# Sample rows of a MoE block spread over 128 partitions and gathered by two row halves of TensorE

## The chip, the cores and the metric

The kernel runs on one core of a Trainium2 chip. The metric is the device time of one execution in microseconds. The kernel before took 584.08, 584.25 and 587.18 us in three timed runs, median 584.25.

## The reference

One inference step of a two-layer decoder trunk on 256 prompt tokens and 64 sample tokens (8 sequences of 8), model width 1024, everything float32. Layer 0 mixes by sliding-window attention and a diagonal state space model, layer 1 by a gated recurrence and dilated attention. Each layer ends in the same block, a hierarchical mixture of experts over the 320 token rows:

```python
def hier_moe(x, p):                       # x: normed rows, 320 x 1024
    g_idx = argmax(x @ router_g + b_g)    # one of 4 groups
    e_in  = logits of the 4 experts of that group
    top_v, top_i = top_k(e_in, 2)         # 2 of 16 experts for each row
    hid = silu(x @ w_gate[e]) * (x @ w_up[e])     # 1024 -> 256
    y   = sum over the two experts of gate * (hid @ w_down[e])   # 256 -> 1024
```

The change lies in this block alone, and the block runs once in each layer.

## The kernel before

The token rows lie in three tiles: t = 0 and 1 are the prompt's (128 rows each), t = 2 the samples' (64 rows, `ROWS[2]`). `moe_block` has one program for each engine, written out by hand; semaphores alone order them.

- **Norm and store (ScalarE, L1743 to L1752).** For each tile ScalarE squares the residual rows with a sum (L1745), takes the root (L1748), waits for VectorE's reciprocal (L1829), scales the rows into `xn` (L1750) and stores them in DRAM as `x_rows` by one DMA of its own queue (L1752): 128 rows of 4 KB for t = 0 and 1, 64 rows of 4 KB for t = 2. Landings are counted by `first_out` (t = 0 and 1) and `rows_out` (t = 2).
- **Routing (VectorE, TensorE).** Logits, choice of two experts, place of each row in its expert's list of 64 (`CAP`). `place(0, 2)` and `place(2, 3)` (L1911, L1914) write the one-hot matrix `Sf` for the first two experts.
- **First pair of experts.** The 16 experts are worked in 8 pairs j = 0 to 7, 64 rows for each expert of a pair. The rows of pair 0 don't come from DRAM: `gather_first` (L1489) multiplies `xn` by `Sf`, eight products for each tile, all three tiles summed in banks 2 and 3 of PSUM. VectorE moves each bank out with the norm's gain (`first_turned`, L1849) to `xgT`.
- **up, turn_hidden, down.** `up(j)` (L1518) multiplies `xgT` by gate and up weights, two experts side by side on column halves of TensorE, into bank 2 + j % 2. `down(j)` (L1549) writes banks 4 and 5.
- **List of the other pairs.** After `up(0, 0, 2)` TensorE makes the row lists of all pairs (L1618) from `L` (VectorE, L1939) and `H` (GpSimd, L1415). VectorE writes them out as `idx` (L1949). GpSimd then fetches the rows of pair 1 from `x_rows` (`gather(1)`, L1400), which `turn(1)` (L1500) transposes. Before it GpSimd waits for `first_out`, `rows_out`, `idx_ok` and `first_pe`. In layer 0 `turn(1)` comes right after `up(0)`, in layer 1 after `down(0)` (`TURN_LATE`).
- **Weights.** SyncE loads pieces of 1 MB (L1273) as places come free. In the first pair it also waits for `gather_steps`, which GpSimd raises right behind `gather(1)`.

TensorE's queue is in order, so a wait in it holds all that follows:

```python
gather_first(2)
up(0, 0, 2)
pe.wait_ge(H_ok, 1)
pe.wait_ge(S_ok, 1)
...                      # the lists, L1618
up(0, 2, KC)
```

Of the kernel before, what the change touches and what calls it, by code (L numbers as in the profile page):

```python
# [16 lines left out]
P = 128  # L17
# [1169 lines left out]
def moe_block(c, x, layer, parts, items, zeroed, xnT, copies, n_copies):  # L1187
# [52 lines left out]
    def gathered_rows(j):  # L1240

        return m["xg"][(j - 1) % XG]

    def yo_of(j):

        return yo[j // LAST]
# [58 lines left out]
    with nc.Block(no_gpsimd_drain=True) as block:  # L1305
# [88 lines left out]
        @block.gpsimd  # L1394
        def _(pool):
            nc.gpsimd.memset(xn[64:P, 2], 0.0).then_inc(gather_steps, 1)

            def gather(j):

                pool.indirect_dma_start(out=gathered_rows(j), out_offset=None, in_=x["x_rows"],  # L1400
                                        in_offset=bass.IndirectOffsetOnAxis(ap=gather_idx[:, j:j + 1], axis=0),
                                        bounds_check=TOK - 1, oob_is_err=False).then_inc(c.xg_in[(j - 1) % XG], 16)

            def scatter(j):

# [12 lines left out]
            pool.wait_ge(first_out, 32)  # L1418
            pool.wait_ge(rows_out, 16)
            pool.wait_ge(idx_ok, 1)  # L1420
            pool.wait_ge(first_pe, 3)
            gather(1)
            nc.gpsimd.memset(m["zero"][:, 1:2], 0.0).then_inc(gather_steps, 1)
            for j in range(2, 1 + XG):
                gather(j)
            pool.wait_ge(zeroed, 16)
            for j in range(LAST):
                if 1 + XG + j < PAIR_N:
                    pool.wait_ge(xt_pe, j + 1)
                    gather(1 + XG + j)  # L1430
                if j < LAST - 1:
                    scatter(j)

        @block.tensor
        def _(pe):
# [50 lines left out]
            def gather_first(t, first=0, end=KC):  # L1486

                for q in range(first, end):
                    last = nc.tensor.matmul(c.bank[2 + q // 4][:, (q % 4) * P:(q % 4 + 1) * P], xn[0:ROWS[t], t, q * P:(q + 1) * P],  # L1489
                                            m["Sf"][0:ROWS[t], t].rearrange("p e s -> p (e s)"),  # L1490
                                            start=(t == 0 and q % 4 == 0), stop=(t == 2 and q % 4 == 3))
                    if t == 2 and q % 4 == 3 or t == 0 and q == KC - 1:
                        last.then_inc(first_pe, 1)

            def turn(j):

                gathered(pe, j)
                pe.wait_ge(xt_ok, 2 * j)
                for q in range(KC):
# [4 lines left out]
            def up(j, first, end):  # L1504

                w = [[piece(6 * j + 2 * part + i).rearrange("p (k n) -> p k n", n=2 * FF) for part in range(2)] for i in range(2)]
                if first == 0:
                    piece_arrived(pe, 6 * j)
                    piece_arrived(pe, 6 * j + 1)
                    pe.wait_ge(xt_ok, 2 * j + 1)  # L1510
                for q in range(first, end):
                    if q == KC // 2:
                        pe.wait_ge(xt_ok, 2 * j + 2)
                        piece_arrived(pe, 6 * j + 2)
                        piece_arrived(pe, 6 * j + 3)
                    for i in range(2):
                        half = slice(64 * i, 64 * i + 64)
                        last = nc.tensor.matmul(c.bank[2 + j % 2][half, :], xgT[:, j % 2, q, half], w[i][q // 4][:, q % 4, :],  # L1518
                                                start=(q == 0), stop=(q == KC - 1))
# [221 lines left out]
        def _(act):  # L1741
            act.dma_start(m["route_in"], x["route_in"][layer]).then_inc(ld, 16)
            for t, rows in enumerate(ROWS):  # L1743
                act.wait_ge(added, 2 * t + 2)
                nc.scalar.activation(xn[0:rows, t], c.resid[0:rows, t], ACT.Square,  # L1745
                                     accum_out=c.stat[0:rows, t:t + 1]).then_inc(sq_ok, 1)
# [3 lines left out]
                nc.scalar.activation(xn[0:rows, t], c.resid[0:rows, t], ACT.Copy, scale=c.stat[0:rows, 6 + t:7 + t]).then_inc(xn_ok, 1)  # L1750
                act.wait_ge(xn_ok, t + 1)
                act.dma_start(x["x_rows"][t * P:t * P + rows, :], xn[0:rows, t]).then_inc(rows_out if t == 2 else first_out, 16)  # L1752
            act.wait_ge(earg, 1)
# [3 lines left out]
            for j in range(PAIR_N):  # L1757
                act.wait_ge(up_pe, j + 1)
                if j >= 2:
                    act.wait_ge(hid_ok, j - 1)  # L1760
                nc.scalar.activation(sg[:, j % 2], c.bank[2 + j % 2][:, 0:FF], ACT.Silu).then_inc(sg_ok, 1)  # L1761
                act.wait_ge(ht_pe, j + 1)
# [52 lines left out]
        def _(dve):  # L1815
# [29 lines left out]

            def first_turned(h):

                dve.wait_ge(first_pe, h + 2)
                v.tensor_tensor(xgT[:, 0, 4 * h:4 * h + 4, :], c.bank[2 + h][:, :].rearrange("p (k r) -> p k r", k=4),  # L1849
                                c.gains[:, gain, 4 * h:4 * h + 4].unsqueeze(2).broadcast_to([P, 4, P]), ALU.mult).then_inc(xt_ok, 1)  # L1850

# [56 lines left out]
            def place(a, b):  # L1908

                dve.wait_ge(pos_pe, 1 + a // 2)  # L1910
                v.scalar_tensor_tensor(m["tmp"][:, a:b], c.bank[7][:, 16 * a:16 * b].rearrange("p (t e) -> p t e", e=E_N), 1.0,  # L1911
                                       m["sum"][:, a:b], ALU.add, ALU.mult).then_inc(tmp_ok, 1)
                dve.wait_ge(tmp_ok, 1 + a // 2)
# [49 lines left out]
            def hidden(j):  # L1963

                dve.wait_ge(sg_ok, j + 1)
                if j >= 2:
                    dve.wait_ge(ht_pe, j - 1)
                v.tensor_tensor(hid[:, j % 2], sg[:, j % 2], c.bank[2 + j % 2][:, FF:2 * FF], ALU.mult).then_inc(hid_ok, 1)  # L1968

# [972 lines left out]
```

## Time and profile before

| | before |
|---|---|
| median of three timed runs | 584.25 us (584.08, 584.25, 587.18) |
| profiled execution, its own time | 586.33 us |
| its span | 584.1 us |
| TensorE busy | 558.7 us, 96% |
| VectorE, ScalarE, GpSimd busy | 247.0, 155.9, 89.0 us |
| moved by DMA | 208.94 MB, mean 358 GB/s |

The profile is of one execution, whose own time is 2.2 us longer than the span of its instructions. "Busy" is time in which an engine works. A released wait is shown in brackets behind the instruction that it held: the idle time, and who ended it. Line numbers are those of the kernel before.

### The profile page before, as it was taken

The page shows a single profiled execution, that of the slowest core. Times are in us where ns is not written, and L with a number is a line of the kernel's source. Part 1 is how long each engine was busy: PE and PEld are TensorE (multiplying, and loading weights), DVE is VectorE, ACT ScalarE, POOL GpSimd, SP SyncE. Part 2 cuts the span into 40 slices and gives each one's busy share as a digit, 9 for nine tenths or more (in the row PEclk, how much of TensorE's full clock was granted, in tenths as well). Part 3 has the DMA queues.
Part 4 walks back from the last instruction along what each step waited for, and adds up shares of the span by engine and source line. Part 5 has one row for each costly group of instructions (what it writes and reads, how often), then busy time and mean ns, then how long its engine had stood idle before and what let it go on. Part 6 is the DMA issues. An engine that isn't in the chain of part 4 may idle for free. (4 is left out here: it accounts for less than half of the span.)

```text
span 584.1 us, 8477 instructions
## 1 busy us (share of the span) xinstructions
PE 558.7 (96%) x3422; PEld 307.2 (53%) x3422; DVE 247.0 (42%) x558; ACT 155.9 (27%) x328; POOL 89.0 (15%) x116
## 2 busy tenths in 40 slices
PE   5999999999999999998999999999999889999993
PEld 4777876544533333337876556567644533333331
DVE  6999882224651112145633415250113732221146
ACT  7132295121301101134235105163013210101123
POOL 5993800000121110000100001000000012120000
PEclk9999999999899999999999999999999999999997
DMA  8995999996999999999999998999699999999872
GB/s 328 418 358 78 239 390 382 383 417 272 378 388 421 420 421 418 397 295 376 380 416 328 412 397 297 313 354 422 257 421 420 381 364 415 420 420 422 363 235 91
DMA packets 40073, 208.94 MB, mean 358 GB/s; under 512 B 12835, under 2 KB 14563, under 8 KB 24192
## 3 DMA queue, kind: packets, MB, share of 16 engines
q1 hardware_dynamic: 30560, 169.93, 74.5%
q0 software_dynamic: 7872, 34.53, 16.5%
q10 hardware_dynamic: 1600, 3.90, 1.7%
q8 instruction: 29, 0.48, 0.3%
q14 instruction: 12, 0.10, 0.0%
HBM read 198.77 MB, written 43.74 MB: 415 GB/s over the span
## 5 line engine op out<-in xcount | busy, mean ns | idle before, releaser
L1518 PE MATMUL bank<-arena 128*64 128x512 f32 x264 | 87.1, 610 | 0.5 <-DVE arena L1858 0.5
L1518 PE MATMUL bank<-ring,arena 128*64 128x512 f32 x232 | 76.3, 613 | 0.1
L2315 PE MATMUL bank<-arena,ring 128*128 128x320 f32 x256 | 71.6, 434 | 0.0
L2315 PEld LDWEIGHTS bank<-arena,ring 128*128 128x128 f32 x256 | 48.0, 190 | 21.4 <-issue 1.6
L1439 PE MATMUL bank<-ring,arena 128*128 128x512 f32 x92 | 40.3, 594 | 1.0 <-PEq L455 0.6
L1518 PEld LDWEIGHTS bank<-arena 128*64 128x64 f32 x264 | 24.2, 138 | 31.9 <-issue 31.8
L1549 PE MATMUL bank<-arena 128*64 128x512 f32 x136 | 39.8, 594 | 0.7 <-ACT arena L1763 0.7
L577 PE MATMUL bank<-xnT,ring 128*128 128x320 f32 x144 | 39.5, 434 | 0.6 <-DVE xnT L897 0.6
L1974 DVE COPY arena<-bank 128x512 f32<-128x512 f32 x14 | 9.7, 692 | 68.3 <-PE bank L1549 68.3
L1549 PE MATMUL bank<-ring,arena 128*64 128x512 f32 x120 | 36.1, 593 | 0.7 <-ACT arena L1763 0.7
L1518 PEld LDWEIGHTS bank<-ring,arena 128*64 128x64 f32 x232 | 21.1, 139 | 25.2 <-issue 25.0
L577 PEld LDWEIGHTS bank<-xnT,ring 128*128 128x128 f32 x144 | 27.1, 190 | 11.7 <-DVE xnT L897 0.7
L1439 PEld LDWEIGHTS bank<-ring,arena 128*128 128x128 f32 x92 | 17.2, 190 | 22.7 <-issue 22.7
L1761 ACT ACTIVATE arena<-bank 128x256 f32<-128x256 f32 x16 | 6.1, 384 | 84.6 <-PE bank L1518 84.6
L1408 POOL DMA_INDIRECT y_rows<-arena x12 | 12.1, 1007 | 107.2 <-DVE arena L1974 107.2
L1968 DVE TENSOR_TENSOR arena<-arena,bank 128x256 f32<-128x256 f32 x16 | 6.7, 422 | 49.0 <-ACT arena L1761 49.0
L1858 DVE TENSOR_TENSOR arena<-bank,small 128x512 f32<-128x512 f32 x28 | 18.0, 686 | 22.1 <-PE bank L1500 19.6
L1766 ACT COPY arena<-bank 128x512 f32<-128x512 f32 x16 | 9.4, 586 | 65.0 <-PE bank L1549 65.0
L1549 PEld LDWEIGHTS bank<-arena 128*64 128x64 f32 x136 | 12.4, 136 | 20.7 <-issue 20.1
L2371 PE MATMUL bank<-ring,arena 128*128 128x512 f32 (+1 forms) x64 | 21.2, 489 | 0.0
L1745 ACT ACTIVATE arena<-resid 128x1024 f32<-128x1024 f32 (+1 forms) x6 | 6.3, 1058 | 54.0 <-DVE resid L1824 54.0
L1549 PEld LDWEIGHTS bank<-ring,arena 128*64 128x64 f32 x120 | 11.4, 136 | 16.1 <-issue 15.7
(450 smaller groups left out, 851.7 us busy)
## 6 DMA issues: line engine op xcount, KB each, us to landing
arena<-in_w_moe SPq DMA_DIRECT2D x50, 1024.0 KB, 16.4
ring<-in_w_moe SPq DMA_DIRECT2D x44, 1024.0 KB, 15.0
arena<-in_stream_b SPq DMA_DIRECT2D x4, 2560.0 KB, 15.0
out_o_d_old<-in_cache_d_g POOLq DMA_DIRECT2D x1, 8448.0 KB, 29.8
arena<-in_stream_a SPq DMA_DIRECT2D x4, 2048.0 KB, 10.4
out_o_d_old<-in_cache_d_g POOLq DMA_DIRECT2D x1, 7680.0 KB, 40.7
out_o_d_old<-in_cache_d_g SPq DMA_DIRECT2D x1, 4608.0 KB, 38.2
ring<-in_w_out_even SPq DMA_DIRECT2D x2, 2048.0 KB, 11.2
```

What stands on the lines that cost most here:

```text
L577: last = nc.tensor.matmul(bank(name)[:, 0:TOK], lhs(k), c.xnT[:, k, :], start=(k == 0), stop=(k == KC - 1))
L1408: pool.indirect_dma_start(out=x["y_rows"], out_offset=bass.IndirectOffsetOnAxis(ap=scatter_idx[:, j:j + 1], axis=0), in_=yo_of(j), in_offs ...
L1439: last = nc.tensor.matmul(c.bank[2 * t + h][:, :], parts[q][:, t * P:(t + 1) * P], where[q][:, h * 512:(h + 1) * 512], start=(q == 0), sto ...
L1518: last = nc.tensor.matmul(c.bank[2 + j % 2][half, :], xgT[:, j % 2, q, half], w[i][q // 4][:, q % 4, :], start=(q == 0), stop=(q == KC - 1))
L1549: last = nc.tensor.matmul(c.bank[4 + h][half, :], hidT[:, j % 2, f, half], w[i][:, f, h * 512:(h + 1) * 512], start=(f == 0), stop=(f == 1))
L1745: nc.scalar.activation(xn[0:rows, t], c.resid[0:rows, t], ACT.Square, accum_out=c.stat[0:rows, t:t + 1]).then_inc(sq_ok, 1)
L1766: nc.scalar.copy(yo_of(j)[:, 0:512], c.bank[4][:, :]).then_inc(yo_a, 1)
L1858: v.tensor_tensor(xgT[:, j % 2, 4 * h:4 * h + 4, :], c.bank[h][:, :].rearrange("p (k r) -> p k r", k=4), c.gains[:, gain, 4 * h:4 * h + 4] ...
L1968: v.tensor_tensor(hid[:, j % 2], sg[:, j % 2], c.bank[2 + j % 2][:, FF:2 * FF], ALU.mult).then_inc(hid_ok, 1)
L1974: v.tensor_copy(yo_of(j)[:, 512:D], c.bank[5][:, :]).then_inc(yo_b, 1)
L2315: last = nc.tensor.matmul(bank(name)[:, 0:TOK], w[:, k, i * P:(i + 1) * P], xnT[:, k, :], start=(k == 0), stop=(k == KC - 1))
L2371: last = nc.tensor.matmul(bank(f"v{2 * t + n}")[:, 0:m], xnT[:, k, t * P:(t + 1) * P], wv[:, k, c0:c0 + m], start=(k == 0), stop=(k == KC ...
```

## The change

The samples' 64 normed rows are no longer 64 partitions of 1024 columns: the first 512 columns stand on partitions 0 to 63 and the last 512 on partitions 64 to 127, both in columns 0 to 511 of `xn[:, 2]`. `tmp` and with it `Sf[:, 2]` get a copy on partitions 64 to 127. `gather_samples` takes the place of `gather_first(2)`: the same eight products, but in pairs, one on the upper and one on the lower 64 rows of TensorE, for bank 2 and bank 3. The square goes to `xgT`, the scaling is two instructions of 64 x 512, and the store is two DMAs of 64 rows of 2 KB. `first_turned` is in three parts (columns 0 to 1, 2 to 3, 4 to 7 of eight), and the first of them releases `up(0, 0, 2)`, which now writes bank 4.

```diff
-            nc.gpsimd.memset(xn[64:P, 2], 0.0).then_inc(gather_steps, 1)
+            nc.gpsimd.memset(xn[:, 2], 0.0).then_inc(gather_steps, 1)
...
-            pool.wait_ge(rows_out, 16)
+            pool.wait_ge(rows_out, 32)
...
+    def up_bank(j):
+        return 2 + j % 2 if j else 4
...
+            def gather_samples():
+                for q in range(4):
+                    for h in range(2):
+                        half = slice(64 * h, 64 * h + 64)
+                        last = nc.tensor.matmul(c.bank[2 + h][:, q * P:(q + 1) * P], xn[half, 2, q * P:(q + 1) * P],
+                                                m["Sf"][half, 2].rearrange("p e s -> p (e s)"), start=False, stop=(q == 3))
+                        if q == 3:
+                            last.then_inc(first_pe, 1)
...
                 if first == 0:
-                    pe.wait_ge(xt_ok, 2 * j + 1)
+                    pe.wait_ge(xt_ok, 2 * j + 2 if j else 1)
                 for q in range(first, end):
+                    if j == 0 and q == 2:
+                        pe.wait_ge(xt_ok, 2)
...
-            pe.wait_ge(xn_ok, 3)
-            gather_first(2)
+            pe.wait_ge(xn_ok, 4)
+            gather_samples()
...
+                else:
+                    act.wait_ge(gather_steps, 1)
+                    for h in range(2):
+                        nc.scalar.activation(xn[64 * h:64 * h + 64, 2, 0:512], c.resid[0:64, 2, h * 512:(h + 1) * 512], ACT.Copy,
+                                             scale=c.stat[0:64, 8:9]).then_inc(xn_ok, 1)
+                    act.wait_ge(xn_ok, 4)
+                    for h in range(2):
+                        act.dma_start(x["x_rows"][SEQ:TOK, h * 512:(h + 1) * 512], xn[64 * h:64 * h + 64, 2, 0:512]).then_inc(rows_out, 16)
...
+            v.memset(m["tmp"][64:P, 2], 0.0)
...
+                if a == 2:
+                    v.scalar_tensor_tensor(m["tmp"][64:P, 2, 0:2], c.bank[7][0:64, 32:34], 1.0, m["sum"][0:64, 2, 0:2], ALU.add, ALU.mult)
...
-            first_turned(0)
-            first_turned(1)
+            first_turned(0, 2)
+            first_turned(2, 4)
+            first_turned(4, KC)
```

## Rows read from the trace of the kernel before

**Rows 1.** The page: the span, and busy time of each engine.
```profile
span 584.1 us, 8477 instructions
PE 558.7 (96%) x3422; PEld 307.2 (53%) x3422; DVE 247.0 (42%) x558; ACT 155.9 (27%) x328; POOL 89.0 (15%) x116
```

**Rows 2.** Timeline, layer 0: start us, length us, engine, line; idle time before it.
```profile
152.04 2.05 PE L1489 MATMUL bank<-arena 64*128 64x128 f32 x16 [0.68 <-DVE arena L1914]
153.30 1.51 DVE L1849 TENSOR_TENSOR arena<-bank,small 128x512 f32<-128x512 f32 x2 [0.39 <-PE bank L1489]
154.73 0.95 DVE L1939 TENSOR_TENSOR arena<-arena 128x768 bf16<-128x768 f32 x1
...
157.96 0.17 DVE L1949 TENSOR_SCALAR arena<-bank 128x16 uint32<-128x16 f32 x1 [1.32 <-PE bank L1618]
159.16 1.12 POOL L1400 DMA_INDIRECT arena<-x_rows,arena  x1 [6.83 <-issue]
163.16 0.86 PEld L1500 LDWEIGHTS bank<-ident,arena 128*128 128x128 f32 x8 [0.81 <-DMA arena<-x_rows,arena]
```

**Rows 3.** Timeline of PE alone, 153 to 164 us.
```profile
154.14 3.36 PE L1518 MATMUL bank<-arena 128*64 128x512 f32 x8
157.43 0.49 PE L1618 MATMUL bank<-arena 128*128 128x16 bf16 x12
157.85 5.38 PE L1518 MATMUL bank<-arena 128*64 128x512 f32 x24
```

**Rows 4.** PE in stretches: busy us, count, granted clock, DMA share, GB/s.
```profile
154.50:157.90 3.40, 3.40 (x22) 0.50 1.02 427
465.20:468.60 3.40, 3.35 (x9) 0.51 1.03 431
473.50:476.60 3.10, 1.44 (x8) 1.00 1.01 418
```

**Rows 5.** Chain that ended last, layer 1: start us, length us, what.
```profile
463.18 2.05 PE bank L1489 x16
465.28 3.53 PE bank L1518 x8
468.81 0.39 PE bank L1618 x12
```

**Rows 6.** Timeline, layer 1.
```profile
465.87 0.95 DVE L1939 TENSOR_TENSOR arena<-arena 128x768 bf16<-128x768 f32 x1
480.19 1.09 PE L1500 MATMUL bank<-ident,arena 128*128 128x128 f32 x8
```

**Rows 7.** Timeline: 64-row products in two row halves, and small operations.
```profile
67.80 1.16 PE L647 MATMUL bank<-arena 64*128 64x128 f32 x16
147.15 0.76 DVE L1836 TENSOR_TENSOR xnT<-bank,small 128x256 f32<-128x256 f32 x2 [0.55 <-PE bank L1458]
141.99 0.26 DVE L1894 SCALAR_TENSOR_TENSOR arena<-arena 128x16 f32<-128x16 f32 x2
148.34 1.15 ACT L1750 ACTIVATE arena<-resid,stat 64x1024 f32<-64x1024 f32 x1 [0.23 <-DVE stat L1829]
149.52 0.51 ACTq L1752 DMA_DIRECT2D x_rows<-arena  x1
169.04 0.59 ACT L1766 COPY arena<-bank 128x512 f32<-128x512 f32 x1 [3.95 <-PE bank L1549]
```

**Rows 8.** DMA issues at 125, 149.5 and 159 us: KB, us to landing.
```profile
x_rows<-arena ACTq DMA_DIRECT2D x1, 512.0 KB, 8.6
...
x_rows<-arena ACTq DMA_DIRECT2D x1, 256.0 KB, 7.3
...
arena<-x_rows,arena POOLq DMA_INDIRECT x1, 3.9
```

**Rows 9.** DMA queues, 153.4 to 156.9 us: packets, MB, share of 16 engines.
```profile
q1 hardware_dynamic: 164, 1.21, 82.2%
q10 hardware_dynamic: 80, 0.26, 18.5%
```

More of the change, by code:

```diff
@@ L1488, in gather_first @@
                 for q in range(first, end):
[L1489 to L1492, printed above, removed]
+                    last = nc.tensor.matmul(c.bank[2 + q // 4][:, (q % 4) * P:(q % 4 + 1) * P], xn[:, t, q * P:(q + 1) * P],
+                                            m["Sf"][:, t].rearrange("p e s -> p (e s)"), start=(t == 0 and q % 4 == 0), stop=False)
+                    if t == 0 and q == KC - 1:
                         last.then_inc(first_pe, 1)
+            def gather_samples():
[6 more added lines that the diff above has]
+                            last.then_inc(first_pe, 1)
             def turn(j):
                 gathered(pe, j)
-                pe.wait_ge(xt_ok, 2 * j)
+                pe.wait_ge(xt_ok, 2 * j + 1)
                 for q in range(KC):
@@ L1509, in up @@
                     piece_arrived(pe, 6 * j + 1)
-                    pe.wait_ge(xt_ok, 2 * j + 1)
+                    pe.wait_ge(xt_ok, 2 * j + 2 if j else 1)
                 for q in range(first, end):
+                    if j == 0 and q == 2:
+                        pe.wait_ge(xt_ok, 2)
                     if q == KC // 2:
-                        pe.wait_ge(xt_ok, 2 * j + 2)
+                        pe.wait_ge(xt_ok, 2 * j + 3)
                         piece_arrived(pe, 6 * j + 2)
@@ L1517, in up @@
                         half = slice(64 * i, 64 * i + 64)
-                        last = nc.tensor.matmul(c.bank[2 + j % 2][half, :], xgT[:, j % 2, q, half], w[i][q // 4][:, q % 4, :],
+                        last = nc.tensor.matmul(c.bank[up_bank(j)][half, :], xgT[:, j % 2, q, half], w[i][q // 4][:, q % 4, :],
                                                 start=(q == 0), stop=(q == KC - 1))
@@ L1744, in _ @@
                 act.wait_ge(added, 2 * t + 2)
-                nc.scalar.activation(xn[0:rows, t], c.resid[0:rows, t], ACT.Square,
+                nc.scalar.activation(xn[:, t] if t < 2 else xgT[0:64, 0].rearrange("p k m -> p (k m)"), c.resid[0:rows, t], ACT.Square,
                                      accum_out=c.stat[0:rows, t:t + 1]).then_inc(sq_ok, 1)
@@ L1749, in _ @@
                 act.wait_ge(rstd_ok, t + 1)
-                nc.scalar.activation(xn[0:rows, t], c.resid[0:rows, t], ACT.Copy, scale=c.stat[0:rows, 6 + t:7 + t]).then_inc(xn_ok, 1)
-                act.wait_ge(xn_ok, t + 1)
-                act.dma_start(x["x_rows"][t * P:t * P + rows, :], xn[0:rows, t]).then_inc(rows_out if t == 2 else first_out, 16)
+                if t < 2:
+                    nc.scalar.activation(xn[:, t], c.resid[:, t], ACT.Copy, scale=c.stat[:, 6 + t:7 + t]).then_inc(xn_ok, 1)
+                    act.wait_ge(xn_ok, t + 1)
+                    act.dma_start(x["x_rows"][t * P:(t + 1) * P, :], xn[:, t]).then_inc(first_out, 16)
+                else:
[6 more added lines that the diff above has]
+                        act.dma_start(x["x_rows"][SEQ:TOK, h * 512:(h + 1) * 512], xn[64 * h:64 * h + 64, 2, 0:512]).then_inc(rows_out, 16)
             act.wait_ge(earg, 1)
@@ L1760, in _ @@
                     act.wait_ge(hid_ok, j - 1)
-                nc.scalar.activation(sg[:, j % 2], c.bank[2 + j % 2][:, 0:FF], ACT.Silu).then_inc(sg_ok, 1)
+                nc.scalar.activation(sg[:, j % 2], c.bank[up_bank(j)][:, 0:FF], ACT.Silu).then_inc(sg_ok, 1)
                 act.wait_ge(ht_pe, j + 1)
@@ L1844, in logits_out, with first_turned @@
                 v.tensor_copy(m["lgT"][:, t * P:t * P + ROWS[t]], c.bank[5][:, t * P:t * P + ROWS[t]]).then_inc(lt_ok, 1)
[L1846 to L1850, printed above, removed]
+            def first_turned(k0, k1):
+                dve.wait_ge(first_pe, 2 + k0 // 4)
+                v.tensor_tensor(xgT[:, 0, k0:k1, :], c.bank[2 + k0 // 4][:, k0 % 4 * P:(k0 % 4 + k1 - k0) * P].rearrange("p (k r) -> p k r", r=P),
+                                c.gains[:, gain, k0:k1].unsqueeze(2).broadcast_to([P, k1 - k0, P]), ALU.mult).then_inc(xt_ok, 1)
             def xg_turned(j):
@@ L1910, in place @@
                 dve.wait_ge(pos_pe, 1 + a // 2)
-                v.scalar_tensor_tensor(m["tmp"][:, a:b], c.bank[7][:, 16 * a:16 * b].rearrange("p (t e) -> p t e", e=E_N), 1.0,
-                                       m["sum"][:, a:b], ALU.add, ALU.mult).then_inc(tmp_ok, 1)
+                if a == 2:
+                    v.scalar_tensor_tensor(m["tmp"][64:P, 2, 0:2], c.bank[7][0:64, 32:34], 1.0, m["sum"][0:64, 2, 0:2], ALU.add, ALU.mult)
+                rows = P if a == 0 else 64
+                v.scalar_tensor_tensor(m["tmp"][0:rows, a:b], c.bank[7][0:rows, 16 * a:16 * b].rearrange("p (t e) -> p t e", e=E_N), 1.0,
+                                       m["sum"][0:rows, a:b], ALU.add, ALU.mult).then_inc(tmp_ok, 1)
                 dve.wait_ge(tmp_ok, 1 + a // 2)
@@ L1967, in hidden @@
                     dve.wait_ge(ht_pe, j - 1)
-                v.tensor_tensor(hid[:, j % 2], sg[:, j % 2], c.bank[2 + j % 2][:, FF:2 * FF], ALU.mult).then_inc(hid_ok, 1)
+                v.tensor_tensor(hid[:, j % 2], sg[:, j % 2], c.bank[up_bank(j)][:, FF:2 * FF], ALU.mult).then_inc(hid_ok, 1)
             def pair_end(j):
```

## The prediction

> **What bounds the kernel now.** I read the page's busy times first: TensorE works 558.7 of 584.1 us [rows 1], and it is one queue in order, so what moves a waiting point of it moves the end. The chain that ended last, in order of time, confirms it for layer 1: samples' gather, `up(0, 0, 2)`, the lists, the rest of `up(0)`, one behind the other [rows 5]. Then I read the timeline of the same stretch in layer 0 [rows 2, 3], the stretches with their granted clock [rows 4], and last the DMA issues [rows 8, 9].
>
> Three things are to be seen there.
> - The samples' gather is 16 matmul records in 2.05 us, started by `Sf` (L1914). VectorE begins on bank 2 at 153.30, when half of them are done, and `up(0)` starts at 154.14 [rows 2, 3].
> - The first 8 records of `up(0)` take 3.36 us in layer 0 and 3.53 us in layer 1 [rows 3, 5]. Twenty-four take 5.38, that is 0.435 us for each of 12 pairs once the last record's 0.59 is off. Eight should take 4 x 0.435 + 0.15 = 1.9. The granted clock was 0.50 there, the lower of the two levels (1.2 against 2.4 GHz), right behind the 64-row gather [rows 4]. The gather itself had no break. In another stretch, 473.50 to 476.60, it was busy only 1.44 of 3.10 us and kept 1.00 [rows 4].
> - In layer 0 `turn(1)` is released by the landing of `gather(1)`: issued 159.16, 3.9 us to landing, 163.1, and TensorE's first weight load of it is at 163.16 [rows 2, 8]. TensorE itself was ready at the same moment (the last of 12 pairs starts at 157.85 + 11 x 0.435 = 162.6, and 0.55 later is 163.2). So there are two chains with no slack between them. In layer 1 `turn(1)` is at 480.19 [rows 6]; the rows are there by 468.8 + 5.7 = 474.5, with 5.7 the distance from lists to landing in layer 0.
>
> **The state of the timed runs.** The profiled execution took 586.33, 2.1 above the median, and the three runs are two near 584.2 and one 587.18. The half clock costs 1.46 us in layer 0 (4 x 0.435 after 154.14 less one pair, 155.44, plus 0.53 to the lists gives 155.97, against 157.43) and 1.65 in layer 1 (465.28 and the same 1.83 give 467.11; the chain has the lists from 468.81, shown some 0.05 late) [rows 3, 5]. Together 3.1 us, and 587.18 less 584.17 is 3.0. I take it that two of the three runs had full clock there and one had not. That is inference: no row shows an unprofiled run's clock. The sum is made for both.
>
> **The change part by part.**
>
> *Gather in halves.* The row for it is L647: 16 records of the same form, 64 rows by 128 columns, on two row halves and two banks, in 1.16 us [rows 7]. So 2.05 becomes 1.16, that is 0.89 less. If halves did not overlap it would stay 2.05, and both banks would end late (rival 4). But `up(0)` doesn't wait for the end of the gather, only for bank 2 and its evacuation: bank 2 is now whole some 1.1 us after the start instead of 1.2. So about 0 is gained here by itself; what goes is TensorE's own end at 154.09, which would have held any earlier `up`.
>
> *Evacuation in three.* The first part is 128 x 256 instead of 128 x 512. Two of 128 x 256 take 0.76, so 0.38 to 0.42 each, against 1.51/2 = 0.755 [rows 2, 7]: `up(0)` is released 0.35 earlier. The three together take 0.4 + 0.4 + 0.75 = 1.55 against 1.51, so VectorE goes on to `L` 0.04 later. The second part is there 0.4 behind the first; `up(0, 0, 2)` needs 1.9, so it hides it. The bank change (4 for 2) only lets this overlap be; bank 4 is read out long before.
>
> *The copy of `tmp`.* One more small operation ahead of L1911: two such take 0.26 where a small one by itself takes 0.17 (L1949) [rows 2, 7], so 0.09 on the path to `Sf`. It delays gather, evacuation and `L`. The memset of `tmp` is smaller still and stands far ahead, where VectorE waits for logits; with no such cover it would be 0.1 more.
>
> *ScalarE.* One scaling of 1.15 becomes two of 64 x 512; the nearest row is 0.59 for 128 x 512 [rows 7]. So 1.18, and `xn` is ready at 149.6, 2.4 us before TensorE asks for it. The square in `xgT` costs nothing, nor does the wait for a memset that is first in GpSimd's program. The second store's issue is at most 0.5 more of ScalarE's queue [rows 7], and the next there, an Exp, waits for VectorE's work behind `L`.
>
> Sum to the lists: `up(0)` starts 0.35 - 0.09 = 0.26 to 0.28 earlier with the bank's small gain. At half clock the lists follow `up`, so 0.28 a layer. At full clock they would follow `L` instead: before, `up` lets them start at 155.97 while `L` ends at 154.73 + 0.95 = 155.68; after, `up` gives 155.69 and `L`, 0.13 later, 155.81 and a release of 0.05. The gain is then only 0.12 a layer. In layer 1 the numbers are 467.11 against 466.95 [rows 6], so again about 0.12 to 0.15.
>
> *The store in two.* The 64 rows are now 128 pieces of 2 KB in place of 64 of 4 KB, on the same queue. Bytes are equal, so the lower bound is 0. For the upper: in 153.4 to 156.9 the store's queue (q10) held 18.5% of 16 engines for 80 packets, 64 of them of 4 KB, which makes 0.16 us each; q1 with 82.2% for 164, some 16 of them tiny, 0.31 each [rows 9]. If an engine takes the two queues in turn, each of the store's pieces costs 0.16 + 0.31 = 0.47, four for each engine now. Four more turns at that are 1.9. At 2 KB (0.08 + 0.31) eight turns are 3.1 against 1.9, and one more completion write, 0.3: 1.5. The nearest rows are the landings under load: 128 rows of 4 KB took 8.6, 64 rows 7.3 [rows 8], 1.3 for four more turns. I take 1.3.
>
> What it is worth: before, `rows_out` was whole at 149.52 + 7.3 = 156.8, and `idx` was written at 157.96 + 0.17 = 158.13; GpSimd's fetch started 1.03 later. So it was hidden by 1.3 us. After, it lands at 158.1 to 158.2 in both states.
> - Half clock: `idx` at 157.85, fetch at 158.13 + 1.03 = 159.16, as before. Layer 0 gains nothing: the 0.28 of `up` turns into a wait of `turn(1)`. Layer 1 keeps its 0.28. Sum 586.33 - 0.28 = 586.05.
> - Full clock: before, `idx` at 156.67 and rows at 156.8, fetch 157.8, landed 161.75, TensorE ready at 161.70: a tie. After, landed 163.1, TensorE ready at 161.6 and idle 1.5 us. Layer 0 loses 1.35. Layer 1 gains 0.12 (its `turn(1)` has 5 us of room, and the late landing costs nothing). Sum +1.2: 584.25 + 1.2 = 585.45.
>
> The wait added (`rows_out` 32 for 16) stands in GpSimd's queue ahead of `gather(1)`, of `gather_steps`, for which SyncE's weight loads of the first pair wait, and of `gather(2)`. These slide by 1.3 too at full clock; `turn(2)` slides with them, and the weights so loaded are pieces 19 and on, for pair 3 and later.
>
> The Trainium skill ("DMA: Bandwidth & Descriptors", Queues, rings and completion order) says that a DMA engine drains a whole packet of some 9 to 17 descriptors from one ring before it turns to the next. By that the store's smaller pieces would go out together and little would be added; the measured landings above, 1.3 later for four more pieces an engine, stand between this and strict turns. It is weighed as rival 1.
>
> **The rivals.**
> 1. *The store lands no later* (under 0.3). For: same bytes, and the second issue, 0.5 at most, may be hidden in the 7.3 to landing. Against: the 1.3 between 128 and 64 rows. Then full clock gives 0.12 + 0.12: 584.0; half clock 586.33 - 0.56. Chance 0.23.
> 2. *The clock stays up where it fell.* The fall came right behind 2.05 us of matmuls on half of the rows; now both halves work together, and `up` starts sooner. If the median run had the fall in it after all (the profile has), layer 1 keeps 1.63 and 0.12 in place of 0.28; layer 0 is bound by the store and gains nothing. Sum 584.25 - 1.75 = 582.5; with rival 1 too, -3.3 = 580.9. For: both falls stand behind that gather and none behind longer idle time. Against: the spread of the three runs. Chance 0.15.
> 3. *The clock falls in more runs* (the slower side). TensorE now idles: 0.9 less work in the gather, and at full clock 1.5 us before `turn(1)`, followed by a stretch of transposes and waits up to `down(0)`. If the clock falls in the median run where it did not, at two places, it is 1.2 + 3.1 = 4.3, 588.5; at one, 1.2 + 1.6, 587.05. [...] Against: one stretch with less than half busy kept 1.00 [rows 4]. The Trainium skill ("TensorE: Matmul & The Clock Gate", Part 1) ties the clock to how busy the engine was, and names idle stretches alone as the danger; by that the shorter gather would speak for this rival, but here the fall came behind a stretch busy throughout. Chance 0.12.
> 4. *The halves don't overlap.* Bank 2 whole at 154.2, `up` at 154.7: 0.55 later in each layer. With the store: 584.25 + 1.35 + 0.55 = 586.1. Against: L647. Chance 0.04.
>
> The forecast, the store's landing taking the place of the lists in layer 0, has the remaining 0.46.
>
> **How the numbers follow.** Likeliest 585.4, its own range 584.6 (store 0.5 later) to 586.2 (store 1.9 later, at full clock). The whole range 582.4 to 587.0 leaves out the far part of rivals 2 and 3. A change below 0.5%, 2.9 us, is about what a measurement of this kernel can't tell from none, so the bounds are 581.3 and 587.2. Faster needs rivals 2 and 1 together, or both falls gone: 0.06. Slower needs rival 3 at two places or beside another mishap: 0.09. The rest, 0.85, is no change that can be told.
>
> **What would show it.** The gather 16 records in 1.2 us, and L1849 in three instructions with the first near 0.4. `up(0)` about 0.28 us nearer to the row of L1911 than before. Landings of the two stores near 8 to 9 us after issue, `gather(1)` 1 us behind the later one and not behind `idx`, and in layer 0 `turn(1)` released by its DMA with a gap of over 1 us on TensorE if the clock is 1.00 before it. I am wrong if the stores land within 7.5 us, or if the stretch behind the gather is at 1.00 in the profile and the span has dropped by over 2 us.

## The result, and the profile after

| | before | after |
|---|---|---|
| median | 583.74 us (581.97 to 587.18, 10 runs) | 588.38 us (585.42 to 590.76, 10 runs) |
| profiled execution, its own time | 586.33 us | 588.18 us |
| its span | 584.1 us | 586.2 us |

The ratio is 1.0068 [1.005, 1.0086]: slower by 0.7%, and the median lies above the forecast range, which ended at 587.0. (In brackets behind a ratio stands its 95% interval.) Two more series of the changed kernel gave 1.0080 [1.0052, 1.0109] and 1.0045 [1.0022, 1.0069]. The mean of its 28 runs in all three series is 587.75 us, that of the 111 runs of the kernel before that were taken beside the experiments is 584.41, so the change costs 3.3 us where 1.2 was forecast. The mean granted clock of these runs is 0.9935 before and 0.9909 after. One run of one version below (after_4k_delay_both, 594.64 us) was in a slower state and is left out of its ratio and its clock.

The page after, against [rows 1]: TensorE has 2.7 us less work, and the span is 2.1 us longer.

```profile
span 586.2 us, 8489 instructions
PE 556.0 (95%) x3422; PEld 306.4 (52%) x3422; DVE 247.8 (42%) x564; ACT 156.4 (27%) x330; POOL 86.8 (15%) x116
```

The timeline of the changed kernel in layer 0, against [rows 2, 3, 7] (start us, length us, engine, line; in brackets the idle time before it and who ended it):

```profile
148.90 1.47 ACT L1772 ACTIVATE arena<-resid,stat 64x512 f32<-64x512 f32 x2 [0.23 <-DVE stat L1853]
150.40 1.15 ACTq L1776 DMA_DIRECT2D x_rows<-arena  x2
152.39 0.38 DVE L1942 TENSOR_TENSOR arena<-arena 128x128 f32<-128x128 f32 x1
152.83 1.16 PE L1503 MATMUL bank<-arena 64*128 64x128 f32 x16 [0.91 <-DVE arena L1942]
154.09 1.35 DVE L1873 TENSOR_TENSOR arena<-bank,small 128x256 f32<-128x256 f32 x3 [0.40 <-PE bank L1503]
154.66 1.94 PE L1533 MATMUL bank<-arena 128*64 128x512 f32 x8 [0.67 <-DVE arena L1873]
...
157.17 0.16 DVE L1978 TENSOR_SCALAR arena<-bank 128x16 uint32<-128x16 f32 x1
159.71 1.12 POOL L1404 DMA_INDIRECT arena<-x_rows,arena  x1 [6.81 <-DMA x_rows<-arena]
```

The gather takes 1.16 us, the first products of `up(0)` 1.94 at full clock, and `idx` is written at 157.33. `gather(1)` starts 2.4 us later, at 159.71, and what ended its idle time is the store. The later of the two stores landed at 158.79; in the kernel before, all rows were there at 156.78.

Layer 1 has the same wait, and the transposes of `turn(1)` (L1513) come long behind it, with TensorE busy ahead of them:

```profile
471.93 1.10 POOL L1404 DMA_INDIRECT arena<-x_rows,arena  x1 [6.13 <-DMA x_rows<-arena]
...
480.66 1.09 PE L1513 MATMUL bank<-ident,arena 128*128 128x128 f32 x8
```

The same line in the kernel before, released by `idx`:

```profile
470.39 1.10 POOL L1400 DMA_INDIRECT arena<-x_rows,arena  x1 [6.69 <-DVE arena L1949]
```

PE in stretches, changed kernel, against [rows 4] (stretch, its length, PE busy, granted clock, DMA share, GB/s):

```profile
154.50:157.90 3.40, 3.24 (x26) 1.00 1.02 421
263.30:265.20 1.90, 0.47 (x4) 1.00 1.05 448
265.30:268.60 3.30, 3.30 (x12) 0.50 0.78 335
467.20:469.20 2.00, 1.87 (x8) 1.00 1.01 410
```

Both falls behind the gather are gone (154.5 and 467.2 at 1.00), and there is a new one at 265.3. That is the start of the next norm, where TensorE had waited for ScalarE: 0.47 us of work in the 1.9 us ahead of it. Beside such stretches every execution has half clock in its last 4 to 10 us; that tail is not counted as a fall below.

**The measure that made the rest readable.** Span against span says little here, since a fall of the clock moves it as much as the change does. I cut each profiled execution at five events instead: r, the first product of the out projection, in layer 0 and 1 (L1439 before, L1443 after); g, the start of `gather(1)`; s, the first transposes of the next norm (L1680, L1695); and the end. All in us:

| | r to g, layer 0 | g to s | s to r | r to g, layer 1 | g to end |
|---|---|---|---|---|---|
| before | 46.14 (half clock) | 105.42 | 162.31 | 43.50 (half clock) | 113.76 |
| after | 46.13 | 105.58 | 163.75 (half clock) | 42.88 | 114.32 |
| before_three_parts | 44.97 | 105.47 | 162.78 | 41.93 | 113.91 |
| after_4k_store | 44.78 | 105.34 | 162.17 | 41.92 | 113.69 |
| before_delay_l1 | 44.86 | 105.21 | 162.54 | 44.61 (half clock) | 114.41 |
| before_delay_both | 45.73 | 105.25 | 163.27 | 42.93 | 114.65 |
| after_four_stores | 48.89 | 107.00 (half clock) | 162.16 | 45.70 | 116.98 |

"Half clock" marks a piece with a stretch of it in that execution. What is to be seen: from `gather(1)` to the end of the layer is nearly fixed, 105.2 to 105.6 and 113.7 to 114.7 (105.05 to 106.1 and 113.67 to 114.65 over all executions but those of experiments 3, 4 and 7), whatever the clock did before it, save where the gather is very late. So the end of each layer follows the start of `gather(1)`; experiments 7 and 8 test whether it is the cause. The profiled execution of the kernel before has its gather as late as the changed kernel in layer 0 (46.14), since `up(0)` ran at half clock there.

### The profile page after: what moved, and what is told of

The parts are those of the page before. It is cut to its first block and busy times, and to the rows that moved or that the text cites. A ratio compares the mean times of both kernels' runs of the same rounds, so it can differ in the third digit from the quotient of the medians.

```text
span 586.2 us, 8489 instructions
## 1 busy us (share of the span) xinstructions
PE 556.0 (95%) x3422; PEld 306.4 (52%) x3422; DVE 247.8 (42%) x564; ACT 156.4 (27%) x330; POOL 86.8 (15%) x116
## 5 line engine op out<-in xcount | busy, mean ns | idle before, releaser
L1533 PE MATMUL bank<-arena 128*64 128x512 f32 x264 | 85.6, 598 | 1.1 <-DVE arena L1873 0.7
L1533 PE MATMUL bank<-ring,arena 128*64 128x512 f32 x232 | 74.7, 598 | 0.7 <-DVE arena L1873 0.7
L1443 PE MATMUL bank<-ring,arena 128*128 128x512 f32 x92 | 40.3, 594 | 1.0 <-PEq L455 0.6
L1564 PE MATMUL bank<-arena 128*64 128x512 f32 x136 | 39.8, 594 | 0.7 <-ACT arena L1787 0.7
L1564 PE MATMUL bank<-ring,arena 128*64 128x512 f32 x120 | 36.1, 593 | 0.7 <-ACT arena L1787 0.7
L1443 PEld LDWEIGHTS bank<-ring,arena 128*128 128x128 f32 x92 | 17.2, 190 | 22.7 <-issue 22.7
```

Source lines behind the costliest of these rows:

```text
L1443: last = nc.tensor.matmul(c.bank[2 * t + h][:, :], parts[q][:, t * P:(t + 1) * P], where[q][:, h * 512:(h + 1) * 512], start=(q == 0), sto ...
L1533: last = nc.tensor.matmul(c.bank[up_bank(j)][half, :], xgT[:, j % 2, q, half], w[i][q // 4][:, q % 4, :], start=(q == 0), stop=(q == KC - 1))
L1564: last = nc.tensor.matmul(c.bank[4 + h][half, :], hidT[:, j % 2, f, half], w[i][:, f, h * 512:(h + 1) * 512], start=(f == 0), stop=(f == 1))
```

## Experiments

**1. The store by itself.** Kernel before, with only the samples' store in two:

```diff
-            pool.wait_ge(rows_out, 16)
+            pool.wait_ge(rows_out, 32)
...
+                    for h in range(2):
+                        act.dma_start(x["x_rows"][SEQ:TOK, h * 512:(h + 1) * 512], xn[0:64, 2, h * 512:(h + 1) * 512]).then_inc(rows_out, 16)
```

> The kernel before with one edit: the samples' 64 normed rows are stored by two DMAs of 64 rows of 2 KB instead of one of 64 rows of 4 KB. Store theory (the later landing holds gather(1): in layer 0 it holds TensorE at turn(1), in layer 1 it holds the weight loads behind gather(1), whose stream ends last): later store lands 1.3 to 1.6 us later than in the kernel before, gather(1) some 1.3 us later in layer 0 and 0.9 in layer 1 where the clock is 1.00, time +1.5 to +2.5 us. Clock theory (what costs is the half clock that falls in other places since the gather is shorter): the gather is as before, so no change, within 0.7 us. VectorE theory (the copy of tmp and three parts): no change.

586.87 us, ratio 1.0036 [1.0013, 1.0059], mean clock 0.9912. That is 2.1 us above the kernel before by the ratio and 2.6 by the medians, for the store alone. The rows are there at 158.20 in place of 156.78. Its `gather(1)` in layer 0 has the same releaser as after:

```profile
159.12 1.12 POOL L1400 DMA_INDIRECT arena<-x_rows,arena  x1 [6.81 <-DMA x_rows<-arena]
```

**2. Everything but the split store.** The changed kernel, with the samples' rows scaled whole on 64 partitions, stored by one DMA of 4 KB rows, and the second half scaled once more onto partitions 64 to 127:

```diff
-                    act.wait_ge(xn_ok, 4)
-                    for h in range(2):
-                        act.dma_start(x["x_rows"][SEQ:TOK, h * 512:(h + 1) * 512], xn[64 * h:64 * h + 64, 2, 0:512]).then_inc(rows_out, 16)
+                    nc.scalar.activation(xn[0:64, 2], c.resid[0:64, 2], ACT.Copy, scale=c.stat[0:64, 8:9]).then_inc(xn_ok, 1)
+                    act.wait_ge(xn_ok, 3)
+                    act.dma_start(x["x_rows"][SEQ:TOK, :], xn[0:64, 2]).then_inc(rows_out, 16)
+                    nc.scalar.activation(xn[64:P, 2, 0:512], c.resid[0:64, 2, 512:D], ACT.Copy, scale=c.stat[0:64, 8:9]).then_inc(xn_ok, 1)
```

> The changed kernel with the store of before: ScalarE scales the 64 rows at full width onto partitions 0 to 63, stores them by one DMA of 64 rows of 4 KB, and then scales columns 512 to 1023 once more onto partitions 64 to 127 for the lower row half. Gather in halves, evacuation in three and the copy of tmp stay. Store theory: gather(1) goes back behind idx, time within 0.7 us of the kernel before (583.2 to 584.4), perhaps 0.3 below. Clock theory: stays near 588.4, since the gather is still 1.16 us. VectorE theory: stays near 588.4.

584.94 us, 1.0013 [0.9997, 1.0029], clock 0.9932. The row halves, the copy of `tmp` and the three parts cost nothing that can be told, and bring nothing either. `gather(1)` starts 2.1 us earlier than after, still released by the rows, which here landed at 156.71; the next norm has 0.79 us of idle time ahead where the changed kernel has 1.52, and the clock did not fall in this execution before its tail.

```profile
157.62 1.12 POOL L1404 DMA_INDIRECT arena<-x_rows,arena  x1 [5.47 <-DMA x_rows<-arena]
262.96 1.09 PE L1695 MATMUL bank<-ident,arena 128*128 128x128 f32 x8 [0.79 <-ACT arena L1813]
```

**3. Four stores of 1 KB rows** in the changed kernel (`rows_out` 64, columns in steps of 256), the suspected cost doubled:

```diff
-                    for h in range(2):
+                    for h in range(4):
```

> The changed kernel with the suspected cost doubled: the samples' rows stored by four DMAs of 64 rows of 1 KB. Store theory: 8 more pieces for each DMA engine and two more completions, landing some 2 to 3 us later than in the changed kernel; both layers slide by that, +3 to +5 us, 591.5 to 593.5. Clock and VectorE theories: no change, 588.4.

596.0 us, 1.0209 [1.0178, 1.0239]. The rows land at 161.26 in layer 0, 2.5 later than after, and `gather(1)` follows in both layers:

```profile
162.18 1.12 POOL L1404 DMA_INDIRECT arena<-x_rows,arena  x1 [9.58 <-DMA x_rows<-arena]
477.04 1.09 POOL L1404 DMA_INDIRECT arena<-x_rows,arena  x1 [8.96 <-DMA x_rows<-arena]
```

This costs 8 us more than two stores: 2.8 in each layer from r to g, and also 1.4 and 2.7 behind g (table), less the fall at 265 which this run hasn't; it has one of 6.8 us at 167.4 instead, so the 1.4 is not the late gather alone. Here the weight stream had run dry: the DMA share is 0.03 from 161.4 to 164.0.

**4. One DMA of 128 pieces from all 128 partitions**, in the hope of a quicker form:

```diff
+                    act.dma_start(x["x_rows"][SEQ:TOK, :].rearrange("r (h c) -> h r c", h=2), xn[:, 2, 0:512]).then_inc(rows_out, 16)
```

> The changed kernel with the samples' rows stored by one DMA of 128 pieces of 2 KB from 128 partitions instead of two DMAs. Store theory: as many pieces but one issue and one completion less; it lands 0.5 to 1.0 us earlier than the later of the two stores, and the time is 1 to 1.5 us below the changed kernel's (586.9 to 587.4). Piece size alone, not the second issue: lands as late, 588.4. Clock and VectorE theories: 588.4.

606.55 us, 1.0374 [1.0352, 1.0397], much the slowest: the same 256 KB land some 16 us after issue (an estimate from the start of the gather, which comes 0.9 us behind the landing in the other runs).

```profile
167.03 1.12 POOL L1404 DMA_INDIRECT arena<-x_rows,arena  x1 [14.35 <-DMA x_rows<-arena]
487.98 1.09 POOL L1404 DMA_INDIRECT arena<-x_rows,arena  x1 [14.09 <-DMA x_rows<-arena]
```

The Trainium skill ("DMA: Bandwidth & Descriptors", Why a DMA increments its semaphore by 16 and not by 1) has a DMA spread over as many engines as divide its slowest dimensions, 16 at most. This pattern's slowest dimension is 2, so it would go over two engines. The trace agrees: while only this store was left, the DMA share was 0.13, and two of 16 engines are 0.125 (stretch, its length, PE busy, granted clock, DMA share, GB/s):

```profile
161.00:165.00 4.00, 1.07 (x6) 1.00 0.13 50
```

**5. The three parts by themselves** (kernel before, `first_turned(0, 2)`, `(2, 4)`, `(4, KC)`, `up(0)` in bank 4), and the changed kernel again beside it.

```diff
-            first_turned(0)
-            first_turned(1)
+            first_turned(0, 2)
+            first_turned(2, 4)
+            first_turned(4, KC)
```

> The kernel before with the evacuation in three parts and bank 4 for up(0) alone: no row halves, no copy of tmp, the store of before. VectorE theory as forecast: up(0) starts 0.27 us earlier if TensorE is free by then; its own gather ends at 154.09 and holds it, so 0.0 to 0.1 earlier, and L is 0.04 to 0.1 later; time within 0.3 us of the kernel before. If the three parts cost something by themselves (the part of the change's price that the store does not explain), +0.5 to +1.5 us.

583.57 us, 1.0003 [0.9988, 1.0017], clock 0.9948. Nothing. In its profile the stretch behind the full gather of 2.05 us kept its clock, where [rows 4] has 0.50:

```profile
154.50:157.90 3.40, 3.40 (x28) 1.00 1.03 434
```

> The changed kernel as it is, for a comparison on the same chip as the next three. 587.5 to 589, that is 3.3 to 4.5 us over the kernel before; granted clock of the whole run 0.991 in the mean, where the kernel before has 0.993.

587.71 us, 1.0080 [1.0052, 1.0109]; in this execution the fall behind the gather was there again, at 154.3.

**6. Take TensorE's wait before `turn(1)` away.** In the changed kernel TensorE idles 1.69 us there in layer 0. `TURN_LATE` puts `down(0)` ahead of it, so that TensorE no longer waits for the gather:

```diff
-TURN_LATE = (False, True)
+TURN_LATE = (True, True)
```

> The changed kernel with TURN_LATE set for layer 0 too: turn_hidden(0) and down(0) come before turn(1), so the fetch has 4 us more. Store theory: the 1.7 us gap of TensorE before turn(1) goes, but two small gaps come (about 1.0 before turn_hidden(0), 0.5 before up(1)): 0.5 to 1.0 us less in layer 0, granted clock of the run back near 0.993, time 586.5 to 587.8. If the gap before turn(1) is of no account: +0.8.

587.49 us, 1.0071 [1.0057, 1.0086], clock 0.9906. No gain that can be told against 1.0080 [1.0052, 1.0109] beside it. The gap became two smaller ones, 1.01 us before `turn_hidden(0)` and 0.45 before `up(1)`, so by itself this doesn't clear TensorE's wait; the pair with experiment 10, below, does.

**7. Take the weights from behind the gather.** SyncE's wait for `gather_steps` in layer 1 of the changed kernel moved behind its next wait:

```diff
-                if j == 0:
+                if j == 0 and layer == 0:
                     sp.wait_ge(gather_steps, 2)
...
+                if j == 0 and layer == 1:
+                    sp.wait_ge(gather_steps, 2)
```

> The changed kernel, but in layer 1 SyncE's first weight loads of the pair loop no longer wait for gather(1); the wait stands behind down(0). Stream theory (in layer 1 the price is paid through the weight stream that starts behind gather(1), whose end sets the end): the stream starts up to 1.5 us earlier, the span from gather(1) to the end shrinks from 114.3 to 112.8 to 113.5, time 0.8 to 1.5 us below the changed kernel. TensorE theory (gather(1) is late for turn(1)): no gain, or a loss, since gather(1) now shares the queues.

587.11 us, 1.0049 [1.0030, 1.0067], against 1.0080 in the same session. From g to the end it took 112.75, the only run under 113.6. That points at the weights; the totals' intervals overlap, and by themselves they don't show it. The DMA share bears it out: behind the late gather of the changed kernel it falls to 0.63 over 3 us, and here, with a gather as late (43.1 us from r), it stays near 1. First the changed kernel, then this run:

```profile
472.00:475.00 3.00, 2.96 (x14) 1.00 0.63 205
```

```profile
474.00:477.00 3.00, 2.19 (x12) 1.00 0.98 371
```

**8. Delay the gather alone.** The kernel before, nothing of the change in it; GpSimd first clears the gather's target (0.95 us), so that `gather(1)` starts 1 us later. In layer 0 alone, in layer 1 alone, in both:

```diff
+            nc.gpsimd.memset(gathered_rows(1), 0.0).then_inc(gather_steps, 1)
+            pool.wait_ge(gather_steps, 2)
...
-                    sp.wait_ge(gather_steps, 2)
+                    sp.wait_ge(gather_steps, 3)
```

> The kernel before with one edit in layer 0: GpSimd fills the tile that gather(1) writes with zeros (128 x 1024, some 0.95 us) right before gather(1). Nothing of the store, of TensorE or of VectorE changes; gather(1) is issued 1.0 to 1.3 us later. Stream theory (each layer's end follows the issue of gather(1) at a fixed distance, 105.4 us to the next norm's transposes in layer 0 and 113.8 to the end in layer 1): +1.0 to +1.3, and up to 1 us more from half clock if the longer idle time of TensorE is what brings it. If another part of the change carries the price: within 0.4 of before.

> The same delay in layer 1 alone. Stream theory: +1.0 to +1.3, although turn(1) has 5 us of room there, and no more half clock than before (0.994 in the mean). TensorE theory (only a fetch that TensorE waits for costs): 0.

> The kernel before with GpSimd's fill ahead of gather(1) in both layers: gather(1) 1.1 later twice, no second store. Lateness theory: +2.2 to +2.8 us, as the split store, mean clock 0.993 if the half clock belongs to the second store, 0.991 if it belongs to the lateness in both layers.

Layer 0: 585.32 us, 1.0021 [0.9999, 1.0043]; layer 1: 585.39, 1.0034 [1.0013, 1.0054]; both: 589.0, 1.0068 [1.0045, 1.0091]. Layer 1, where `turn(1)` has its 5 us of room [rows 6] and nothing on TensorE waits, costs no less than layer 0, whose interval by itself reaches just below 1. Both together cost as much as the change, with one store and no row halves. The single delays go with a clock of 0.9933 and 0.9924, both together with 0.9894. The gather, in before_delay_both:

```profile
158.46 1.12 POOL L1400 DMA_INDIRECT arena<-x_rows,arena  x1 [0.88 <-POOL arena L1422]
469.90 1.09 POOL L1400 DMA_INDIRECT arena<-x_rows,arena  x1 [0.82 <-POOL arena L1422]
```

**9. Crossings**, to see whether the parts add anything beside a late gather: after_4k_store with both delays; before_three_parts with the split store; the changed kernel a third time.

> The changed kernel with the one 4 KB store, and the same fill in both layers. If row halves and lateness add up plainly: +2.3 to +2.8 us over before. If they work together (a shorter gather and a longer idle time bring more half clock): +3.5 to +4.5, mean clock 0.991, as the changed kernel.

> The kernel before with the evacuation in three parts and the split store, without row halves and copy of tmp. If the rest of the price is the row halves' and the copy's: +2 us, as the split store alone. If it is the split store with three parts: +3.5 to +4.5.

> The changed kernel on this chip: +3.5 to +4.5 us over before, mean clock 0.991.

1.0055 [1.0029, 1.0080], 1.0048 [1.0029, 1.0066] and 1.0045 [1.0022, 1.0069], with clocks of 0.9904, 0.9914 and 0.9908. One group: all three have `gather(1)` late in both layers, by different means.

**10. A version that might beat both**: three parts, one 4 KB store, and the weights freed as in 7, in layer 1 or in both layers (then with `TURN_LATE` in both).

> The kernel before with evacuation in three parts, and in layer 1 the first weight loads of the pair loop not held for gather(1) (the wait stands behind down(0)). The hold is short here (up_mid comes some 0.5 to 1 us before it), so 0.5 to 1.0 us below the kernel before by the stream theory, 582.6 to 583.1; nothing by the TensorE theory.

> The same in both layers, with TURN_LATE in layer 0 too, so that the fetch has 4 us more there. Stream theory: 1 to 2 us below the kernel before, 581.6 to 582.6. If the fetch in the full queues now comes too late even for the later turn(1), or the two gaps of TURN_LATE cost: no gain or up to +1.

584.33 us, 1.0006 [0.9986, 1.0025], and 583.49 us, 0.9995 [0.9977, 1.0014]. Neither beats the kernel before. With the gather on time, freeing the weights gains nothing, from g to end 113.90 and 113.67: the stream had no hole to close.

## Why the prediction was wrong

The direction was as forecast, later by the store's landing, and the size was not: 1.2 us on the sum, 3.3 measured. The first step already held only half: TensorE was taken for the one engine that sets the end, although the DMA share in [rows 4] is 1.01 to 1.03.

**The gather in halves: right.** 1.16 us as forecast. VectorE begins on bank 2 at 1.26 us from the gather's start in both kernels (152.04 to 153.30, 152.83 to 154.09), so it brings nothing by itself, as said. Rival 4 is out.

**Three parts: nearly right.** `up` starts 0.57 us behind VectorE's start (154.09 to 154.66) where it was 0.84 (153.30 to 154.14): 0.27 gained, 0.35 forecast.

**The copy of `tmp`: too small.** Forecast 0.09. TensorE's wait for `Sf` is 0.91 instead of 0.68, so 0.23; the copy (L1937) and a slower `Sf` (L1942, 0.38 for 0.30) are both in it. That takes back nearly all of the 0.27.

**ScalarE: too small, and on the path.** 1.47 us, not 1.18, and the first store is issued 0.3 us further behind the norm's statistics than before (150.40 - 148.70 against 149.52 - 148.14). The second store's issue comes another 0.5 us later.

**The landing: right.** 2.0 us later by the clock of the span, 1.45 with the later start of that stretch taken off, and 1.42 in experiment 1; 1.3 was taken, 1.9 was the end of the range. The Trainium skill's rule of draining a ring's packet of 9 to 17 descriptors before the next ("DMA: Bandwidth & Descriptors", Queues, rings and completion order), on which rival 1 stood, is not what these traces show. In the kernel before, the 64 pieces of 4 KB start in rounds of 16 that are 0.46 us apart (the rounds begin at 153.64, 154.10 and 154.56), which is one of the store's (0.16) and one of the weights' (0.31) in turn. The trace doesn't name the engine of a piece, so the turns are inferred from the rounds. By the landing, rival 1 is out.

**Layer 0: the size right, the reason wrong.** From r to g it is 46.13, 46.24 and 46.20 in the changed kernel's three executions, against 44.7 to 45.0 where the gather was on time at full clock: 1.2 to 1.5 us, 1.35 forecast. But I had it pass through TensorE's idle time before `turn(1)`, from a tie to 1.5 us. That idle time is 1.69 and 1.42 us in two of the three executions (the third had half clock and none), and 0.83 to 1.12 where the gather was on time. Experiment 6 and the last version of experiment 10 make a pair that shows the loss without that wait. TensorE's start times agree to 0.04 us up to 171.8, with the same two gaps, and it waits for the gather in neither:

```profile
162.96 0.44 PE L1546 MATMUL bank<-ident,arena 128*128 128x128 f32 x2 [1.01 <-DVE arena L1997]
162.93 0.44 PE L1537 MATMUL bank<-ident,arena 128*128 128x128 f32 x2 [1.01 <-DVE arena L1975]
```

Yet s comes at 264.72 in the first and at 263.18 in the second, where the gather was on time and the weights didn't wait for it. What differs in the two traces is the weight stream: with a late gather SyncE's next loads are held, and the DMA engines run dry for about 1 us. The same stretch of experiment 6, of the last version of experiment 10, of the changed kernel and of after_4k_store:

```profile
160.00:163.00 3.00, 1.99 (x11) 1.00 0.58 175
160.00:163.00 3.00, 1.99 (x11) 1.00 0.99 395
160.00:163.00 3.00, 2.29 (x12) 1.00 0.64 199
160.00:163.00 3.00, 2.17 (x14) 1.00 1.02 395
```

A share of 0.64 for 1.02 over 3 us is 1.1 us of all DMA engines, and from 180 to 240 us the changed kernel's share is 1.02. The same hole stands in layer 1, also where only the gather was moved (before_delay_l1):

```profile
469.00:472.00 3.00, 3.00 (x17) 1.00 0.26 107
```

**Layer 1: the step that failed.** The words were: "its `turn(1)` has 5 us of room, and the late landing costs nothing", and of the weight loads behind `gather_steps`: "the weights so loaded are pieces 19 and on, for pair 3 and later". They are late-used, but the stream that brings them is full from then on, and what it lost it doesn't make up. SyncE's waits between 470 and 565 us, the changed kernel (queue, line, who ended it: us in all, times, longest):

```profile
SPq L1298 <- DMA y_rows<-arena: 22.4, 2, 12.5
SPq L1277 <- PE bank L1564: 22.0, 4, 5.7
SPq L1277 <- PE bank L1533: 15.8, 5, 4.7
SPq L1344 <- POOL arena L1427: 9.6, 1, 9.6
```

The last one is the wait in the pair loop: SyncE stands 9.6 us for GpSimd's step behind `gather(1)`. From then the DMA engines have no slack. Changed kernel, stretches as above:

```profile
500.00:520.00 20.00, 20.00 (x98) 1.00 1.01 421
520.00:540.00 20.00, 20.00 (x102) 1.00 1.02 420
540.00:550.00 10.00, 10.00 (x51) 1.00 1.02 422
```

TensorE reads 20.00 of 20.00 too, and that misled me: the ends of matmuls are modelled in these profiles, so a full reading doesn't say that TensorE is at its peak. Which of two full engines sets the end is told by the chain's last steps. Kernel before (start us, length us, what):

```profile
541.49 3.46 PE bank L1549 x16
546.52 8.92 DMA y_rows<-arena
555.52 7.70 DMA arena<-y_rows
```

The changed kernel:

```profile
541.95 3.46 PE bank L1564 x16
546.99 9.02 DMA y_rows<-arena
556.09 9.33 DMA arena<-y_rows
```

Before_delay_l1, where only the gather was moved:

```profile
540.45 3.46 PE bank L1552 x16
545.48 8.95 DMA y_rows<-arena
554.51 9.42 DMA arena<-y_rows
```

Counted from r of layer 1 (426.89 before, 429.05 after), TensorE's last `down` starts at 114.6 before and at 112.9 after: 1.7 us earlier, as two gains and a clock that stayed up should give. The end is at 157.3 and 157.2. What took it back is the load of `y_rows`, 9.33 us for 7.70: it queues behind the weights, whose last packets come at 564.7 before and 566.9 after. With TensorE's last `down` at the earlier time and the gather on time (after_4k_store) that load takes 7.65, and the end is at 155.6. After_four_stores has 14.82. So the late landing costs 1.0 in layer 1 (42.9 for 41.9 from r to g) and nothing behind it gives that back. With the weights freed (experiment 7) the chain's last steps run through TensorE's products in place of that load.

**The clock.** The sum took full clock behind the gather for the median run of the kernel before. The runs fit that: 583.6 to 584.3 as medians of all series, and 583.99 with 0.994 in the profiled execution of before_three_parts. The changed kernel's profile has full clock there too. But the falls don't hang on that gather of 2.05 us on half the rows, as I read [rows 4]: before_three_parts keeps the gather and kept the clock, and after_again fell at 154.3 with the halves. Rival 3, the slower side, is nearest to what came: 587.05 at one further fall, measured 587.75 on the mean. Its mechanism, though, was idle time before `turn(1)`, and with that in two smaller gaps the clock stayed at 0.9906.

What the runs do show is a grouping. Where `gather(1)` is on time in both layers the mean clock is 0.9932 to 0.9948, and 0.9931 to 0.9942 in the four series of the kernel before; late in one, 0.9933 and 0.9924; late in both by 0.5 to 1.5 us, 0.9894 to 0.9914; later still (experiments 3 and 4), 0.9855 and 0.977. The falls in the profiled executions go the same way, counted in stretches of 3.4 us: 2 in the five of versions without a later store or a delay, 9 in the nine of versions that are late in both layers by up to 1.5 us. These are few, and three of the nine had none.

**The sum as measured.** Some 1.3 in layer 0 and 1.0 in layer 1 are 2.3 of the 3.3 us; the other 1.0 is what is left for the clock. Two checks agree. A stretch of 3.4 us at half clock lowers the mean of a 586 us run by 0.0029 and cost some 1.5 us before; the mean is 0.0026 lower, part of that is the tail, which is 0.9 us longer in the changed kernel's profiles (0.0008), and the rest is 0.6 of a stretch in each run, 0.9 us. And runs of equal clock can be compared: with 0.990 or 0.991 the kernel before takes 586.1 us in the mean and the changed kernel 588.1, with 0.992 or 0.993 it is 584.6 and 587.2, so 2.0 to 2.6 us are there whatever the clock. Both are worked out, not the result of an edit.

Why a late gather brings falls is open. Three of the falls come at about 265 us, where TensorE waits for the next norm, and six at 464 to 467 us. The wait at 265 can't be the reason by its length: it is 1.5 to 2.0 us in the changed kernel's executions, but 1.52, 1.94 and 2.08 in three others that had no fall at all.

## What to carry to other kernels

- A late wait is not free because the consumer it feeds has room. List everything that is queued behind it on its engine, above all the semaphore that lets weights go, and look whether the DMA share drops behind the wait and reads full after it. A stream that is full afterwards did not catch up here.
- Where two engines both read 100% busy, take the last three steps of the chain in two executions: the one whose last step grows is behind the stream that sets the end.
- Cut executions at a few named events and compare the pieces; it separates 1 us of a change from 1.5 us of the clock, which whole spans don't.

## What the runs showed of the hardware

- A store of 256 KB beside a full stream of larger pieces lands later the more pieces it has, at equal bytes: 7.3 us behind its first issue as 64 of 4 KB (at 156.8), 8.4 as 128 of 2 KB (158.8), 11.2 as 256 of 1 KB (161.3). Part of it is the issue on ScalarE: 0.51 us for one DMA, 1.15 for two, 2.8 for four in layer 0. The number of DMAs grew with that of pieces, and no run parts the two.
- The same bytes in one DMA whose outermost dimension is 2 went at a DMA share of 0.13, two of 16 engines, and land some 16 us after issue, with the whole kernel 22 us slower.
- A weight stream that is held for 1 us and full afterwards (share 0.58 over 3 us in place of 0.99) ended the layer 1.5 us later, though TensorE's start times had agreed to 0.04 us up to 9 us behind the hole.
- Two ScalarE operations of 64 x 512 take 1.47 us, one of 64 x 1024 takes 1.15. One of the two also writes to other partitions than it reads, which no run parts from their number.
- The granted clock can fall to half (0.50, 1.2 GHz) behind 2.05 us of matmuls without a break, with 0.68 us of idle time ahead of them and none longer in the 4.5 us before the fall; the same kernel does it in one execution and not in the next.
